# Norm sums by a full matrix of ones, with root and inverse 512 wide

## What is computed

```python
def rms_norm(x, g):
    y = x * lax.rsqrt(jnp.mean(x * x, axis=-1, keepdims=True) + EPS)
    return y * g

def modulate(h, shift, scale):
    return h * (1 + scale[:, None, :]) + shift[:, None, :]

# first block, per layer l
h = modulate(rms_norm(x, ffn1_norm[l]), mod[0], mod[1])      # phases f0, f3
h = modulate(rms_norm(x, mix_norm[l]), mod[3], mod[4])       # phases m1, m4
h = modulate(rms_norm(x, ffn2_norm[l]), mod[6], mod[7])      # phases f2, f5
# in the mixer (m1, m4)
q = rms_norm(c_q, q_a_norm) @ w_uq                           # width 384
kv = rms_norm(c_kv, kv_a_norm) @ w_ukv                       # width 256
merged = concatenate([rms_norm(attn, attn_out_norm), rms_norm(conv, conv_out_norm)])   # 512 each
```

## Time and profile before

| | |
|---|---|
| median of 3 runs | 3189.66 us (3188.26 to 3191.57) |
| profiled execution, its own time | 3192.57 us |
| its span, first to last instruction | 3190.8 us |
| mean granted TensorE clock | 0.993 of full speed |
| PE busy | 3134.5 us (98%) |
| DVE busy | 1823.5 us (57%) |
| ACT busy | 1200.4 us (38%) |
| POOL busy | 1020.0 us (32%) |
| DMA, HBM read | 413.10 MB, 132 GB/s over the span |

### The profile page before, as it was taken

How to read it: one execution, slowest core, us unless ns; L and a number is a source line. 1 busy time by engine, 2 the same in 40 slices (tenths; PEclk the granted TensorE clock), 3 DMA queues, 4 the chain that set the end, 5 groups by cost and what they waited for, 6 DMA issues and landing times.

```text
span 3190.8 us, 39673 instructions
## 1 busy us (share of the span) xinstructions
PE 3134.5 (98%) x14521; PEld 2529.3 (79%) x14521; DVE 1823.5 (57%) x2476; ACT 1200.4 (38%) x1810; POOL 1020.0 (32%) x722
## 2 busy tenths in 40 slices
PE   6999999999999999999999999999999999999998
PEld 5888876788888888876788888777888777888887
DVE  6554466665445443366665456446776767475443
ACT  3333245432223222345432233455433342443332
POOL 4995000069911820000069810000799000040000
PEclk8999999999999999999999999999999999999999
DMA  6675333267733643332256634212676344243332
GB/s 239 205 209 146 93 96 103 73 180 209 208 99 120 203 121 93 96 92 57 73 179 209 205 103 134 66 54 67 199 209 192 103 123 105 86 145 92 99 92 93
DMA packets 570955, 420.45 MB, mean 132 GB/s; under 512 B 29237, under 2 KB 531076, under 8 KB 569688
## 3 DMA queue, kind: packets, MB, share of 16 engines
q1 hardware_dynamic: 531940, 287.93, 30.9%
q0 software_dynamic: 35456, 124.01, 13.2%
q10 hardware_dynamic: 3444, 7.02, 0.8%
HBM read 413.10 MB, written 8.68 MB: 132 GB/s over the span
## 4 chain that ended last, share of the span: by engine, by line
PE 90%; DVE 5%; ACT 2%; DMA 1%; issue 1%; SPq 0%; POOL 0%; DVEq 0%; ACTq 0%; POOLq 0%
PE bank L327 27%; PE bank L329 27%; PE bank L328 27%; PE bank L1509 2%; DVE w_lo L308 1%; PE bank L1523 1%; PE bank L1550 1%; DVE tmp L454 1%; DVE h_lo L464 1%; PE bank L361 1%; PE bank L363 1%; PE bank L362 1%; DMA mod_w<-in_w_ada 1%; DVE w_lo L299 1%; PE bank L435 1%
## 5 line engine op out<-in xcount | busy, mean ns | idle before, releaser
L327 PE MATMUL bank<-h_hi,w_hi 128*128 128x512 f32 x2624 | 1034.8, 394 | 8.3 <-DVE w_lo L308 3.7
L329 PE MATMUL bank<-h_hi,w_lo 128*128 128x512 f32 x2624 | 1023.0, 390 | 0.0
L328 PE MATMUL bank<-h_lo,w_hi 128*128 128x512 f32 x2624 | 1022.5, 390 | 0.0
L308 DVE TENSOR_TENSOR w_lo<-raw,w_hi 128x1024 fp32r<-128x1024 f32 x414 | 608.3, 1469 | 578.9 <-ACT w_hi L291 576.4
L291 ACT ACTIVATE w_hi<-raw 128x1024 fp32r<-128x1024 f32 x414 | 437.7, 1057 | 794.0 <-PE bank L329 793.7
L327 PEld LDWEIGHTS bank<-h_hi,w_hi 128*128 128x128 f32 x2624 | 492.2, 188 | 124.0 <-issue 10.1
L329 PEld LDWEIGHTS bank<-h_hi,w_lo 128*128 128x128 f32 x2624 | 491.9, 187 | 106.1
L328 PEld LDWEIGHTS bank<-h_lo,w_hi 128*128 128x128 f32 x2624 | 492.4, 188 | 100.8 <-issue 0.5
L757 POOL TENSOR_TENSOR mod_acc<-mod_acc,mod_w 128x1024 f32<-128x1024 f32 x168 | 444.3, 2645 | 14.7
L327 PE MATMUL bank<-hid_hi,w_hi 128*128 128x512 f32 x1056 | 412.9, 391 | 3.4 <-DVE w_lo L308 2.8
L329 PE MATMUL bank<-hid_hi,w_lo 128*128 128x512 f32 x1056 | 411.1, 389 | 0.0
(11 more groups left out here) (421 smaller groups left out, 3348.4 us busy)
## 6 DMA issues: line engine op xcount, KB each, us to landing
raw<-in_ffn_w_gu SPq DMA_DIRECT2D x176, 512.0 KB, 4.5
mod_w<-in_w_ada POOLq DMA_DIRECT2D x128, 512.0 KB, 3.9
mod_w<-in_mod_w POOLq DMA_DIRECT2D x96, 512.0 KB, 4.2
raw<-in_ffn_w_in SPq DMA_DIRECT2D x88, 512.0 KB, 3.8
raw<-in_ffn_w_down SPq DMA_DIRECT2D x64, 512.0 KB, 3.8
raw<-in_w_in SPq DMA_DIRECT2D x34, 512.0 KB, 3.7
raw<-in_ffn_w_out SPq DMA_DIRECT2D x32, 512.0 KB, 3.8
raw<-in_ffn_w_down SPq DMA_DIRECT2D x32, 384.0 KB, 3.3
```

The lines of the kernel that those rows point to most:

```text
L308: loop(nc.vector.tensor_tensor(w_lo[:, u % 2, :], raw[:, u % 2, :], w_hi[:, u % 2, :].bitcast(F32), ALU.subtract), "split_lo", times)
L327: nc.tensor.matmul(dst, a_hi, b_hi, start=start, stop=False)
L328: nc.tensor.matmul(dst, a_hi, b_lo, start=False, stop=False)
L329: return nc.tensor.matmul(dst, a_lo, b_hi, start=False, stop=stop)
```

## The change

For 16 of the norms (the pair norms of m1, f2, f3, m4, f5, f7, o8, f9, and q, kv, attn, conv of both mixers) the sum is one matmul with the 128x128 matrix of ones as weights and the 512 columns of squares moving. Its result is [128, 512] with the sum of token n in column n of every partition, so nothing needs spreading. The root goes over 512 columns, straight into `inv_rms` (pair, q, attn) or `tmp[:, 3, :]` (kv, conv), and the reciprocal is taken there in place, 512 wide. The spread matmuls and the copy by `pair_act` go (the even phase keeps both). The scale waits for `norm_inverse`, DVE's own. The conv sum has two such matmuls, one for each of its two tiles of squares. f0, b with e6, the heads and the end keep the old form. The order of instructions on each engine is otherwise the same.

```diff
+        def norm_home(key):
+            return tmp[:, 3, :] if key[1] in ("kv", "conv") else inv_rms[:, :]
+
+        def row_sums(pe, bank, squares):
+            for n, sq_n in enumerate(squares):
+                ins = nc.tensor.matmul(psum[bank][:, :], ones[:, :], sq_n, start=n == 0, stop=n == len(squares) - 1)
+            return ins
+
         def norm_sum(pe, key, bank, squares=None):
             wait(pe, "square_added", squares or key)
+            if key != "end" and key[0] != "b":
+                done(row_sums(pe, bank, [total_sq]), "norm_sum", key)
+                return
...
         def norm_root(act, key, bank):
             wait(act, "norm_sum", key)
-            done(nc.scalar.activation(stat[:, 0:TQ], psum[bank][:, 0:TQ], ACT.Sqrt, bias=eps[:, :]), "norm_root", key)
+            if key == "end" or key[0] == "b":
+                root, sums = stat[:, 0:TQ], psum[bank][:, 0:TQ]
+            else:
+                root, sums = norm_home(key), psum[bank][:, :]
+            done(nc.scalar.activation(root, sums, ACT.Sqrt, bias=eps[:, :]), "norm_root", key)
...
         def norm_invert(dve, key):
             wait(dve, "norm_root", key)
-            done(nc.vector.reciprocal(stat[:, TQ:2 * TQ], stat[:, 0:TQ]), "norm_inverse", key)
+            if key == "end" or key[0] == "b" or key == PHASES[0]:
+                inverse, root = stat[:, TQ:2 * TQ], stat[:, 0:TQ]
+            else:
+                inverse = root = norm_home(key)
+            done(nc.vector.reciprocal(inverse, root), "norm_inverse", key)
...
         def pair_act(act, key):
-            wait(act, "norm_spread", key)
-            done(nc.scalar.activation(inv_rms[:, :], psum[4][:, :], ACT.Copy), "inv_ready", key)
+            if key[0] == "e":
+                wait(act, "norm_spread", key)
+                done(nc.scalar.activation(inv_rms[:, :], psum[4][:, :], ACT.Copy), "inv_ready", key)
...
                     if j == 0 and kt == 3:
                         norm_sum(pe, key, 4, squares)
-                    if j == 0 and kt == 5:
-                        norm_spread(pe, key, 4)
...
-            for t in range(TQ):
-                for half in range(2):
-                    ins = nc.tensor.matmul(psum[bank][:, t:t + 1], c_sq[:, half, t * P:(t + 1) * P], ones[:, 0:1],
-                                           start=half == 0, stop=half == 1, skip_group_check=True)
-            done(ins, "conv_sum", key)
+            done(row_sums(pe, bank, [c_sq[:, 0, :], c_sq[:, 1, :]]), "conv_sum", key)
```

More of the change, by code:

```diff
@@ L450, in norm_scale @@
             if m == 0:
-                wait(dve, "inv_ready" if key in LAZY else "norm_spread", key)
+                wait(dve, "norm_spread" if key == PHASES[0] else "inv_ready" if key[0] == "e" else "norm_inverse", key)
             if m >= 3:
@@ L470, in norm_scale_split @@
                     norm_low(dve, key, m - 2, shift, dst_lo, dst_hi)
-                norm_scale(dve, key, psum[bank][:, :], m, src, gain)
+                norm_scale(dve, key, psum[bank][:, :] if key == PHASES[0] else norm_home(key), m, src, gain)
             for m in range(max(0, n - 2), n):
@@ L1658, in pe_out_halves @@
                         conv_sum(pe, key, 4)
-                    if n == 1 and q == 0:
-                        conv_spread(pe, key, 4)
                 unit_end(ins)
@@ L1784, in conv_sum @@
             wait(pe, "conv_squared", (key, 3))
-            for t in range(TQ):
-                for half in range(2):
-                    ins = nc.tensor.matmul(psum[bank][:, t:t + 1], c_sq[:, half, t * P:(t + 1) * P], ones[:, 0:1],
-                                           start=half == 0, stop=half == 1, skip_group_check=True)
-            done(ins, "conv_sum", key)
+            done(row_sums(pe, bank, [c_sq[:, 0, :], c_sq[:, 1, :]]), "conv_sum", key)
         def conv_root(act, key, bank):
             wait(act, "conv_sum", key)
-            done(nc.scalar.activation(stat[:, 16:16 + TQ], psum[bank][:, 0:TQ], ACT.Sqrt, bias=eps[:, :]), "norm_root",
+            done(nc.scalar.activation(norm_home((key, "conv")), psum[bank][:, :], ACT.Sqrt, bias=eps[:, :]), "norm_root",
                  (key, "conv"))
@@ L1797, in conv_invert @@
             wait(dve, "norm_root", (key, "conv"))
-            done(nc.vector.reciprocal(stat[:, 20:20 + TQ], stat[:, 16:16 + TQ]), "norm_inverse",
+            done(nc.vector.reciprocal(norm_home((key, "conv")), norm_home((key, "conv"))), "norm_inverse",
                  (key, "conv"))
-        def conv_spread(pe, key, bank):
-            wait(pe, "norm_inverse", (key, "conv"))
-            done(each_row(bank, 20), "norm_spread", (key, "conv"))
         def conv_take(dve, key, n, u):
@@ L1839, in pe_mla @@
                 if n == 6:
-                    norm_spread(pe, (key, "q"), 5)
                     norm_sum(pe, (key, "kv"), 6)
-                if n == 9:
-                    norm_spread(pe, (key, "kv"), 6)
-                if n == 6:
                     wait(pe, "proj_read", (key, 5))
@@ L1913, in conv_part @@
                         norm_sum(pe, (key, "attn"), 3)
-                    if h == HEADS - 1 and kt == 4:
-                        norm_spread(pe, (key, "attn"), 3)
                 if last == KT:
@@ L2179, in scale @@
             def scale(m):
-                norm_scale(dve, (key, "attn"), psum[3][:, :], m, lambda m: attn[:, m, :], lambda m: col(("attn_out_norm", l), m))
+                norm_scale(dve, (key, "attn"), norm_home((key, "attn")), m, lambda m: attn[:, m, :], lambda m: col(("attn_out_norm", l), m))
             def low(m):
@@ L2184, in scale_conv @@
             def scale_conv(m):
-                norm_scale(dve, (key, "conv"), psum[4][:, :], m, lambda m: conv[:, m, :],
+                norm_scale(dve, (key, "conv"), norm_home((key, "conv")), m, lambda m: conv[:, m, :],
                            lambda m: col(("conv_out_norm", l), m))
```

## The result

The changed kernel takes 3223.9 us (median of four runs, 3223.4 to 3233.0) against 3190.6 for the kernel before beside it: ratio 1.0111, 95% interval 1.0094 to 1.0129. In a later comparison it took 3226.1 us against 3189.4: ratio 1.0118, 1.0103 to 1.0132. So it is 33 to 37 us slower by the medians. The forecast was 3216 in a range of 3204 to 3229: right in sign and inside the range, but some 8 to 10 us too low, and outside its own narrower range of 3210 to 3220.

The account below looks back on a forecast made before the run. PE bounds the kernel (90% of the chain), with DVE's chain pacing it at the norms. DVE delays of +23.1 us plus +3.4 for the clock, sum +26.5, on the median 3189.66 gave 3216 us, range 3204 to 3229.

Parts of the forecast that it names:

- R: Time of one 512-wide reciprocal on DVE at each of the 16 norms, taken as 3.4 us, bounds 0.7 to 3.6.
- Steps 1 to 6: DVE's delays at pairs after mixers +13.2, after feed-forwards +3.5, q nothing, kv +5.0, attn +3.4, conv -2.0: +23.1 us.
- pairs after a mixer: Step 1, pairs f2, f5, f7, f9 (after a mixer or o8): everything behind the reciprocal moves by +3.3 us each, +13.2.
- pairs after a feed-forward: Step 2, pairs m1, f3, m4, o8: two DVE waits absorb part, first `h_lo` +0.87 us later, 4 * 0.9 = +3.5.
- kv, with the lead of 0.7: Step 4, two kv norms: reciprocal delays the bank PE needs by 3.2 us, less PE's 0.7 us lead: 2 * 2.5 = +5.0.
- the 15.3 named: Sign in f2: 15.3 us instead of 11.96 from the reciprocal's start to PE's first product of the second unit.
- Step 7: Clock falls to 1.2 GHz after PE's wait at each of two kv norms: 2 * 1.7 = +3.4 us.
- the third rival: Waits in pairs after mixers and at attn let the clock fall too: 6 * 1.7 = +10 us, 3226; 14%.
- The first rival: DVE's time is covered at the 16 norms, so PE's saved 12.8 us count: 3177 us; 5%.
- The second: Rival of no change: the wide reciprocal streams like a plain operation, 0.7 us, -4 us in all, 3185; 8%.
- the dearer reciprocal: Rival: each wide reciprocal takes 4.4 us by the rule of 8 steps, +12 us, 3228; 7%.
- The one by which the change doesn't do what it says: Rival: a pair's inverse still waits for something of the old chain, time between 3196 and 3211; 6%.

Follow-up runs that it names:

- filled version: The changed kernel with unread 512-column products put into PE's waits at kv, attn and the four pairs after a mixer or o8: 3213.8 us, ratio 1.0077.
- run with 16 columns: The changed kernel with its 16 wide reciprocals over only 16 of 512 columns, output not the reference's: 3180.5 us, ratio 0.9970.
- 256 columns: The changed kernel with its 16 wide reciprocals over 256 of 512 columns, output not the reference's: 3199.9 us, ratio 1.0022.
- kv late: The changed kernel with kv's reciprocal moved behind the steps that free the bank PE waits for: 3212.4 us, ratio 1.0067.

## Why the prediction was right, and where it was short

**R.** Predicted 3.4 us, measured 3.35. The line through 4 and 16 elements was the right one to extend: 252 ns for 16 columns, 1753 for 256, 3353 for 512 give 6.25 ns an element on both stretches, and 152 ns fixed. The Trainium skill's repeat count of 8 ("VectorE: DVE Perf Modes", section "First, the fixed hardware budget"), from which the prediction had estimated 4.4 us as a rival, is too dear by 1 us here; the measurement decides.

**Steps 1 to 6, DVE's delays.** Predicted and measured: pairs after a mixer 3.3 and 3.33; pairs after a feed-forward 0.87 and 0.78; kv, with the lead of 0.7, 2.5 and 3.15-0.75 = 2.4; attn 1.7 and 1.8; conv -1.0 and -0.95 to -0.99 where the clock stayed up. The sum was +23.1. With the measured ones it is 4*3.33+4*0.78+2*(2.40+1.79-0.95) = +22.9. The filled version, which keeps this part alone, measures +25 (20 to 29 by its interval). The root was put at 0.60 us and took 0.69. In the pairs after a feed-forward it was hidden, as said. In those after a mixer it wasn't: it held the reciprocal back by 0.16 us, so that of the 3.33 us the reciprocal made 3.18 and the root the rest, and 3.3 came out in part by luck. Two more readings were off and hardly moved the sum: DVE's waits in a pair after a feed-forward are used up from R = 1.75 us on, not from 2.5, and the root's part at attn is 0.5 us (the reciprocal starts 1.33 us after the split's end instead of 0.82), not 0.34. In f2 the product at 662.41 came 15.1 us after the reciprocal's start instead of the 15.3 named, as the reciprocal itself started 0.16 us later behind the longer root.

**Step 7, the clock: the step that failed in size.** "I take one such fall at each kv: 2 * 1.7 = +3.4". The falls at kv came in all four cases of two profiles, but longer than the one of the earlier trace rows: 6.8 us instead of 3.4, for 2.0, 1.9, 1.8 and 2.7 us, some 4.2 per run. It isn't half of 6.8 because the first part of each fell into the wait itself; the changed kernel's stretch before its product at 472.08 has half clock and no product on PE:

```profile
470.00:472.00 2.00, 0.00 (x0) 0.00 (x0) 1.97 (x4) 0.04 (x1) 0.07 (x1) 0.50 0.00 0
```

And falls came elsewhere, where the sum had none and the prediction named a clock of 1.00 in the pairs as its sign. At attn the clock fell in three of four cases of the changed kernel and in five of eight over all runs with that wait, for some 1.6 us each. In the pairs after a mixer it fell in 12 of 16 cases of four profiles. The argument against it that stood beside the third rival, "PE catches up before DVE has the next split", held for the five falls of 3.4 us, which cost nothing (3.33 with and without), and failed for the seven of 6.8 us, which cost 1.0 to 1.2 us each. Added up, the clock cost 8.2 us in the first profile (kv 3.9, attn 3.1, f5 1.2) and 8.3 in the second (4.5, 1.6, 2.2), where the sum had 3.4. 22.9+8.2 = 31.1 us against a measured 33 with an interval of 30 to 41 in the first comparison, and 37 with 33 to 42 in the second; what lies between can be chance inside o8, and isn't settled.

**The rivals.** The third one, given 14%, named just these places and 3226 us: right in mechanism, and nearer the time than the forecast, the latter in part by luck. It took all six of them at 1.7 us, 10 in all; a fall came at most of them and cost about that much at attn only, and the six together cost 4.3 and 3.8 us in the two profiles. The Trainium skill ("TensorE: Matmul & The Clock Gate", section "HAM oscillation") says that waits between bursts bring the clock down; here, waits of 2.5, 3.0 and 4.8 us were followed by half clock in 12 of 16, 5 of 8 and 4 of 4 cases, and filling them ended it. The first rival, DVE's time covered, has its counterpart in the run with 16 columns: 3180.5, where it was put at 3177. The second, no change by R = 0.7, is out by the reciprocal's row, and so is the dearer reciprocal. The one by which the change doesn't do what it says is out by the pairs: from the reciprocal to the first scale DVE runs without a gap.

**One thing that the prediction left out** is that parts of the kernel's own time come and go. Its rows come from one profile, which held 6.8 us of half clock inside o8 by chance. The forecast of the time doesn't suffer from it, since it adds the sum to the median; a comparison of two profiles place by place does.

## What to carry to other kernels

A reciprocal's cost goes with the elements of one partition, whether the 128 partitions hold new values or the same one: making the sum 128 times over to save PE 0.8 us took the reciprocal from 4 elements to 512, and from 0.17 us to 3.35, and it stood at the head of a chain that PE waits for. Before widening an operation, ask who waits behind it; at kv, moved back by five operations, the same 3.3 us were free. And where a change makes PE's waits longer, price the clock behind each of them besides the wait, from the longest fall that the trace shows (6.8 us inside o8) and not from the shortest (3.4); whether PE can catch up decides if it counts.

## What the runs showed of the hardware

- DVE's reciprocal in fp32: 252, 1753 and 3353 ns for 16, 256 and 512 elements a partition, 6.25 ns each (runs with 16 and 256 columns, changed kernel), where DVE's TENSOR_TENSOR of 512 at L1833 takes 0.67 us.
- ACT's square root of 512 columns of a bank takes 690 ns, 92 more than the copy of the same bank in the earlier trace rows.
- A fall of the granted clock after a wait of PE isn't certain at 2.5 and 3.0 us: the same wait in the same kernel was followed by none, 3.4 or 6.8 us at 1.2 GHz. At 4.8 us (kv) it was followed by 6.8 us in all four cases, at 1.62 us (kv late) by none in both. Inside o8 the clock also falls amid products of few columns, for nothing to 17 us, with no edit near.
- Products whose result nobody reads, issued in the wait, kept the clock at 2.4 GHz at all eight places and delayed nothing; they ended before the wait did.
